# First-layer attention heads placed between value chunks, logarithm-based normalisations and per-tile waits in a two-layer decoder kernel

## The chip, the cores and the metric

The kernel runs on one core of one Trainium2 chip. The metric is the device time of one execution in microseconds (us). The times of before are three runs; a separate execution was profiled, and all rows come from it.

## The reference

Two decoder layers over 512 tokens of width 1024, four heads of 256, everything in float32. The part that the change touches is the attention of layer 0 (stick-breaking), the output projections and the layer normalisations:

```python
# layer 0, per head, s < t only
z = (q @ k.T) / 16
log_1m = where(mask, -softplus(z), 0)
tail = sum over j > s of log_1m[t, j]
a = where(mask, exp(log_sigmoid(z) + tail), 0)
mix = (a @ v) @ w_o
x = layer_norm(alpha * x + mix) * g + b        # three such norms before the last
x = layer_norm(alpha * x + feed_forward(x)) * g + b
x = x + (p @ w_proj) * sigmoid(x @ w_gate)
```

Layer 1 computes a softmax attention with a forget-gate bias, then a top-2-of-8 expert feed-forward with routing.

## The kernel before

All products are made of fp32r halves: a tensor is split into a rounded part (`_hi`) and the remainder (`_lo`), and `mm3` (L706 to L711) issues three matmuls per product. ScalarE (ACT) makes the `_hi` copy, VectorE (DVE) the `_lo` remainder, of weights and of results alike. Weights arrive in chunks through four `raw` buffers on the SP queue (a load waits for the `lo_ready` of the chunk four before it) and are split into two buffers `w_hi`/`w_lo`; chunk c+1 can be split when chunk c-1 has been used.

The phases run in the order of the list `PHASES`: `q0`, `k0`, `v0` (the three projections of layer 0), then the heads of layer 0, `o0` (its output projection), norm 0, `gu` and `down` (feed-forward), norm 1 with the embedding projection `proj0`, `gate0`, then `q1`, `k1`, the heads of layer 1 with the value chunks `v1` between them, `o1`, norm 2, routing, experts, the last gate. Each of `q0`, `k0`, `v0`, `o0`, `q1`, `k1`, `v1`, `o1` has eight chunks. For q, k, o a chunk is one feature tile of 128 (8 x 3 matmuls of 512 columns); for v two chunks make 256 value features (48 matmuls of 256 columns each).

**Heads of layer 0** (TensorE part L866 to L921). The triangle of scores of one head is four key tiles n = 3, 2, 1, 0 of 128, 256, 384 and 512 query columns, in PSUM banks 3 to 0. `scores_a` makes z; ACT computes Abs, Exp and Ln of it into `ln_a` (L1387 to L1392), DVE adds max(z, 0) and multiplies the diagonal blocks by the 0/1 tile `keep` (L1821, L1828); ACT and DVE split the result into `sp_hi`, `sp_lo`; `tails_a` (L891, L895) adds the reverse sums in the same banks; DVE clips the diagonal blocks with `floor_a` (L1838), ACT takes Exp (L1401, L1403), DVE makes `a_hi` and `a_lo` (L1844, L1622), and `mix_a` multiplies by the values. The tiles of this work (`ln_a`, `sp`, `a_hi` and so on) lie in the memory of `x_hi` and `x_lo`, which `v0` reads. TensorE's order is: all of `v0`; scores of head 0; then for each head its tails, the scores of the next head, its mix; then a wait for all eight mixed tiles, and `o0`.

**Heads of layer 1** have the other order already: value chunk 2h, turning the weights of head h, value chunk 2h+1, scores of head h+1, mix of head h. There the causal mask is added in PSUM by one matmul of an identity (`turn_r`) with a tile of large negative numbers (`mask_r`, L987).

**Norms** (ACT from L1305, DVE from L1710). The mean is a matmul (L809, L810), DVE subtracts it, ACT squares (L1311), TensorE averages the squares (L817), ACT takes the square root (L1319), DVE the reciprocal (L1719). Per feature tile DVE multiplies by it (L1725); then ACT writes `x_hi` with gain and bias (L1302) and `x_exact` with gain and bias (L1303), and DVE subtracts the two into `x_lo`. The first two chunks of `gu`, `gate0` and `q1` consume these tiles as they arrive. In norm 1 the splits of `proj0` and `gate0` weights are written between these steps by hand.

In `k1` the DVE step `sides` (L1896 to L1909), five operations on the gate sums and four that make the per-head tiles, sits after the drain of chunk 4. The order on each engine is written out by hand; semaphores alone join the engines.

## Time and profile before

| what | value |
|---|---|
| three runs, median (lowest, highest) | 1445.09 us (1443.63, 1447.59) |
| profiled execution, its time | 1448.43 us |
| its span | 1446.7 us |
| mean granted TensorE clock | 0.956 of full |
| TensorE busy | 1316.7 us, 91% of the span |

The span runs from the first to the last recorded instruction. In a stream of matmuls a row's duration overlaps the next one, so the distance between two starts is what a matmul costs. "Idle before" is the time that an engine stood still, and the arrow names what ended it. A duration of 0.39 us for a 512-column matmul goes with a distance of 0.23 us (clock 2.4 GHz), 0.63 us with 0.43 us (1.2 GHz).

### The profile page before, as it was taken

How to read it: one execution, taken by the hardware profiler on the slowest of the kernel's cores; microseconds unless marked ns; L12 is line 12 of the kernel's file. 1: busy time of each engine (PE TensorE's matmuls, PEld its weight loads, DVE VectorE, ACT ScalarE, POOL GpSimd, SP SyncE). 2: the span in 40 equal slices, each digit the busy share in tenths (PEclk: the TensorE clock that was granted, in tenths of full speed). 3: DMA queues.
4: the chain of work that ended last, by engine and by line, in shares of the span. 5: the costliest groups of instructions: out<-in, count | busy, mean ns of one | idle time of the engine just before them, and what ended most of it. 6: DMA issues, size and time to landing. Idle time of an engine off the chain costs nothing.

```text
span 1446.7 us, 17484 instructions
## 1 busy us (share of the span) xinstructions
PE 1316.7 (91%) x6495; PEld 1102.9 (76%) x6496; DVE 638.7 (44%) x870; ACT 562.2 (39%) x771; POOL 149.7 (10%) x106
## 2 busy tenths in 40 slices
PE   7999879799999999998899999988799899988658
PEld 6889778488888878876786899756687799866547
DVE  5333554633333323336533455344643643354465
ACT  3222552632223222126322233233544644555632
POOL 0000000000000000000000000000333533344400
PEclk9999899999999999999999999997899999988869
DMA  7332003033333333212346431211875866588831
GB/s 187 106 102 78 26 5 98 29 102 87 102 101 87 112 100 100 87 36 74 102 78 65 91 59 44 80 44 73 249 239 173 291 234 196 174 265 261 307 146 59
DMA packets 197911, 175.45 MB, mean 121 GB/s; under 512 B 7200, under 2 KB 178272, under 8 KB 197856
## 3 DMA queue, kind: packets, MB, share of 16 engines
q1 hardware_dynamic: 194016, 160.53, 38.6%
q0 software_dynamic: 3312, 12.06, 2.2%
q10 hardware_dynamic: 528, 2.10, 0.4%
q8 instruction: 37, 0.61, 0.2%
q14 instruction: 18, 0.15, 0.0%
HBM read 164.71 MB, written 9.96 MB: 121 GB/s over the span
## 4 chain that ended last, share of the span: by engine, by line
PE 81%; DVE 6%; issue 6%; ACT 4%; POOL 2%; DMA 1%; POOLq 0%; ACTq 0%; SPq 0%; DVEq 0%
PE bank L709 25%; PE bank L711 24%; PE bank L710 24%; PE bank L817 1%; POOL w_lo L667 1%; DVE w_lo L1622 1%; DVE rstd L1719 1%; PE bank L1026 1%; DMA raw<-moe_w_down 1%; PE bank L891 1%; DMA x_tok<-x 1%; PE bank L895 1%; DVE sp L1821 0%; PE bank L953 0%; DVE a_lo L1622 0%
## 5 line engine op out<-in xcount | busy, mean ns | idle before, releaser
L1622 DVE TENSOR_TENSOR w_lo<-raw,w_hi 128x1024 fp32r<-128x1024 f32 (+5 forms) x215 | 300.4, 1403 | 315.2 <-ACT w_hi L1222 157.5
L709 PE MATMUL bank<-x_hi,w_hi 128*128 128x512 f32 x672 | 265.4, 395 | 17.6 <-DVE x_lo L1622 11.4
L711 PE MATMUL bank<-x_hi,w_lo 128*128 128x512 f32 x672 | 264.0, 393 | 0.0
L710 PE MATMUL bank<-x_lo,w_hi 128*128 128x512 f32 x672 | 263.8, 393 | 0.0
L1222 ACT CAST w_hi<-raw 128x1024 fp32r<-128x1024 f32 (+2 forms) x141 | 149.7, 1063 | 157.5 <-PE bank L711 150.9
L709 PE MATMUL bank<-w_hi,x_hi 128*128 128x256 f32 (+2 forms) x608 | 189.0, 311 | 8.5 <-DVE x_lo L1650 3.2
L710 PE MATMUL bank<-w_lo,x_hi 128*128 128x256 f32 (+2 forms) x608 | 186.5, 307 | 0.0
L711 PE MATMUL bank<-w_hi,x_lo 128*128 128x256 f32 (+2 forms) x608 | 186.4, 307 | 0.0
L709 PEld LDWEIGHTS bank<-x_hi,w_hi 128*128 128x128 f32 x672 | 127.6, 190 | 49.2 <-DVE w_lo L1622 12.1
L1510 ACT CAST w_hi<-raw 128x1536 fp32r<-128x1536 f32 (+2 forms) x98 | 130.3, 1339 | 75.1 <-PE bank L711 47.3
L711 PEld LDWEIGHTS bank<-x_hi,w_lo 128*128 128x128 f32 x672 | 127.4, 190 | 27.2
L710 PEld LDWEIGHTS bank<-x_lo,w_hi 128*128 128x128 f32 x672 | 127.7, 190 | 26.0
L709 PEld LDWEIGHTS bank<-w_hi,x_hi 128*128 128x128 f32 x608 | 115.9, 191 | 12.9 <-issue 9.6
L667 POOL TENSOR_TENSOR w_lo<-raw,w_hi 128x1536 fp32r<-128x1536 f32 (+2 forms) x33 | 103.7, 3141 | 181.4 <-ACT w_hi L1510 136.4
L710 PEld LDWEIGHTS bank<-w_lo,x_hi 128*128 128x128 f32 x608 | 116.0, 191 | 0.0
L711 PEld LDWEIGHTS bank<-w_hi,x_lo 128*128 128x128 f32 x608 | 115.9, 191 | 0.0
L635 POOL IOTA lane_ids<- 128x128 f32 x1 | 0.2, 238 | 910.5 <-DVE q_lo L1650 910.5
L709 PE MATMUL bank<-w_hi,het_hi 128*128 128x512 f32 x132 | 63.0, 477 | 13.4 <-POOL w_lo L667 6.6
L709 PE MATMUL bank<-h_hi,w_hi 128*128 128x512 f32 x176 | 69.3, 394 | 3.2 <-DVE h_lo L1622 3.2
L710 PE MATMUL bank<-h_lo,w_hi 128*128 128x512 f32 x176 | 69.1, 393 | 0.0
L711 PE MATMUL bank<-h_hi,w_lo 128*128 128x512 f32 x176 | 69.0, 392 | 0.0
L1280 ACT CAST x_hi<-x_exact 128x512 fp32r<-128x512 f32 (+1 forms) x24 | 14.9, 621 | 118.1 <-DVE x_exact L1687 118.1
(298 smaller groups left out, 1864.1 us busy)
## 6 DMA issues: line engine op xcount, KB each, us to landing
raw<-moe_w_gu SPq DMA_DIRECT2D x32, 768.0 KB, 4.6
raw<-ffn_w_gu SPq DMA_DIRECT2D x44, 512.0 KB, 3.8
raw<-moe_w_gu SPq DMA_DIRECT2D x32, 640.0 KB, 4.2
raw<-a_w_qkv SPq DMA_DIRECT2D x24, 512.0 KB, 3.7
raw<-moe_w_down SPq DMA_DIRECT2D x16, 768.0 KB
raw<-ffn_w_down SPq DMA_DIRECT2D x16, 704.0 KB, 4.4
raw<-ple_w_gate SPq DMA_DIRECT2D x16, 512.0 KB, 4.1
raw<-kvf_w SPq DMA_DIRECT2D x16, 512.0 KB, 6.9
```

The costliest lines, as they stand in the source:

```text
L667: op = pool.tensor_tensor(w_lo[j][:, 0:n], raw[j][:, 0:n], w_hi[j][:, 0:n].bitcast(F32), ALU.subtract)
L709: pe.matmul(o, s_hi, m_hi, start=start, stop=False, skip_group_check=True)
L710: pe.matmul(o, s_hi, m_lo, start=False, stop=False, skip_group_check=True)
L711: return pe.matmul(o, s_lo, m_hi, start=False, stop=stop, skip_group_check=True)
L817: pe.matmul(bank[5][:, :], mean_f[:, :], sq[k % 2][:, :], start=k == 0, stop=k == KD - 1).then_inc(var_done, 1)
L891: mm = pe.matmul(bank[n][:, 0:WID[n]], neg_incl[:, :], part[:, OFF[n]:OFF[n] + WID[n]], start=False, stop=n == TT - 1 and part is sp_lo, s ...
L895: mm = pe.matmul(bank[n][:, (m - n) * P:WID[n]], neg_ones[:, :], part[:, OFF[m]:OFF[m] + WID[m]], start=False, stop=m == TT - 1 and part i ...
L1026: mm = pe.matmul(bank[5][0:NE, :], w_r[:, k, :], x_exact[:, k, :], start=k == 0, stop=k == KD - 1)
L1222: act.copy(w_hi[j % 2][:, 0:n], raw[j][:, 0:n]).then_inc(hi_ready, 1)
L1280: act.copy(x_hi[:, k, :], x_exact[:, k, :]).then_inc(y_hi_ready, 1)
L1510: op = act.copy(w_hi[j][:, 0:n], raw[j][:, 0:n])
L1622: return dve.tensor_tensor(dst, a, b, ALU.subtract)
```

## The change

- Layer 0's heads take the order of layer 1: `scores_a(0)` follows `k0`; then for each head value chunk 2h, its tails, value chunk 2h+1, the scores of the next head, its mix. The tiles of the head work move out of `x_hi`/`x_lo`, into the part of `q`/`k` memory of the head that is done with it; `ln_a` and `sp_wide` lie in other scratch memory.
- The mask of layer 0 is one more 128-column matmul per score tile (16 in all); the multiplications by `keep` and the clip by `floor_a` are gone. DVE prepares `turn_r` and `mask_r` between `q0` and `k0`.
- Value results: half a group is signalled early (`v_half`), in both layers.
- Norms 0 to 2: square root and reciprocal become Ln (L1319) and Exp with scale -0.5, both on ACT; the table load ahead of the squares stays in norm 1 alone. In norms 0 and 1 the gain goes into the DVE multiplication and the bias into `x_hi` (ACT) and `x_lo` (DVE); `x_exact` gets its bias later: in norm 0 by eight ACT operations within the first four chunks of `gu`, in norm 1 within the gate's addition (DVE).
- `o0` and `o1` wait for each mixed tile ahead of its own first use, in place of one wait for all eight.
- The load of `p` moves behind the loads of `gu` on the SP queue; in `k1` the four per-head operations move from after chunk 4 to after chunk 5.

The diff, cut to its core, with the common indentation taken off:

```diff
@@ -303,16 +306,10 @@
-wk = lambda name, shape, dt, o: at(name, shape, dt, work0 + o)
-ln_a = wk("ln_a", [P, TRI], F32, 0)
-sp = wk("sp", [P, TRI], F32, 5 * KB)
-sp_hi = wk("sp_hi", [P, TRI], R32, 10 * KB)
-sp_lo = wk("sp_lo", [P, TRI], R32, 15 * KB)
-a_hi = wk("a_hi", [P, TRI], R32, 20 * KB)
-a_lo = wk("a_lo", [P, TRI], R32, 25 * KB)
-a_diag = wk("a_diag", [P, TT, P], F32, 30 * KB)
...
+narrow = [[at(f"narrow{h}_{i}", [P, TRI - SEQ], R32, G + 4 * h * KB + 16 * i * KB) for i in range(2)] for h in range(H)]
+wide = [[at(f"wide{h}_{i}", [P, SEQ], R32, G + 4 * h * KB + 32 * KB + 2 * i * KB) for i in range(2)] for h in range(H)]
+sp_narrow = [at(f"sp_narrow{h}", [P, TRI - SEQ], F32, G + 4 * h * KB + 48 * KB) for h in range(H)]
@@ -530,11 +528,11 @@
-load_p(0)
...
+load_p(0)
@@ -765,6 +763,8 @@
+            if mixed_before is not None and isinstance(i, int) and i == j == 0:
+                pe.wait_ge(mix_lo, mixed_before + k + 1)
@@ -773,33 +773,20 @@
-def value_chunk(c):
...
-    weights(BASE["v1"] // RAW + c // RAW, c % RAW)
-    if c and c % 2 == 0:
-        pe.wait_ge(v_ready, 2 * (c // 2))
+def value_chunk(l, c):
...
+    weights(BASE[VALUES[l]] // RAW + c // RAW, c % RAW)
+    if c % 2 == 0 and (l or c):
+        pe.wait_ge(v_ready, 2 * H * l + 2 * (c // 2))
...
+        if t == 1 and c % 2:
+            mm.then_inc(v_half, 1)
...
-def values(name):
...
-    def step(q, i, j, last):
-        weights(q, j)
-        if j % 2 == 0:
-            free_of(DRAINED[name] + (0 if i == 0 and j == 0 else 4 * i + j - 2))
-        for t in range(TT):
-            for k in range(4):
-                w, kk = slice(k * 256, (k + 1) * 256), j % 2 * 4 + k
-                mm = mm3(bank[j // 2 * 4 + t][:, 0:256], x_hi[:, kk, t * P:(t + 1) * P],
-                         x_lo[:, kk, t * P:(t + 1) * P], w_hi[j % 2][:, w], w_lo[j % 2][:, w],
-                         kk == 0, kk == KD - 1)
-        mm.then_inc(chunk_done, 1)
-    quads(pe, name, step)
@@ -867,18 +854,24 @@
-values("v0")
...
 def scores_a(h):
...
+        else:
+            pe.wait_ge(drained, DRAINED["k0"] + 4 + g + 1)
+            pe.wait_ge(masks, 1)
...
-            mm = mm3(bank[n][:, 0:WID[n]], k_hi[:, f, n * P:(n + 1) * P], k_lo[:, f, n * P:(n + 1) * P],
-                     q_hi[:, f, n * P:], q_lo[:, f, n * P:], d == 0, d == DT - 1)
-        mm.then_inc(z_done, 1)
+            mm3(bank[g][:, 0:WID[n]], k_hi[:, f, n * P:(n + 1) * P], k_lo[:, f, n * P:(n + 1) * P],
+                q_hi[:, f, n * P:], q_lo[:, f, n * P:], d == 0, False)
+        pe.matmul(bank[g][:, 0:P], turn_r[:, :], mask_r[:, :], start=False, stop=True,
+                  skip_group_check=True).then_inc(z_done, 1)
...
+def sp_part(h, n, i):
+    return narrow[h][i][:, OFF[n] - SEQ:OFF[n] - SEQ + WID[n]] if n else wide[h][i][:, :]
...
 def tails_a(h):
@@ -904,21 +896,21 @@
-            a = slice(OFF[n], OFF[n] + WID[n])
-            mm = mm3(bank[6 + d][:, n * P:], v_hi[:, n, c], v_lo[:, n, c], a_hi[:, a], a_lo[:, a],
+            if d == 0 and n % 2 == 0:
+                pe.wait_ge(v_ready, 2 * h + n // 2 + 1)
+            mm = mm3(bank[6 + d][:, n * P:], v_hi[:, n, c], v_lo[:, n, c], sp_part(h, n, 0), sp_part(h, n, 1),
...
-        mm.then_inc(mixed, 1)
...
-pe.wait_ge(drained, DRAINED["o0"] - 2)
+    mm.then_inc(mixed, DT)
...
+    value_chunk(0, 2 * h)
...
+    value_chunk(0, 2 * h + 1)
...
-pe.wait_ge(mix_lo, KD)
-tiles("o0", q_hi, q_lo)
+tiles("o0", q_hi, q_lo, mixed_before=0)
@@ -1251,28 +1242,19 @@
-def split_value(c):
-    c += BASE["v1"]
-    split_hi(c // RAW, c % RAW, SIZE["v1"])
...
-def value_hi(g):
...
-    act.wait_ge(chunk_done, BASE["v1"] + 2 * g + 2)
+def split_value(l, c):
+    c += BASE[VALUES[l]]
+    split_hi(c // RAW, c % RAW, KD * P)
...
+def value_hi(l, g):
...
+        if b:
+            act.wait_ge(chunk_done, BASE[VALUES[l]] + 2 * g + 2)
+        else:
+            act.wait_ge(v_half, H * l + g + 1)
...
-def values_hi(name):
-    def step(q, i, j, last):
-        ahead(name, q, j, last)
-        if j % 2 == 0:
-            return
-        act.wait_ge(chunk_done, 4 * q + j + 1)
-        g = 2 * i + j // 2
-        for t in range(TT):
-            op = act.copy(v_hi[:, t, g * 256:(g + 1) * 256], bank[j // 2 * 4 + t][:, 0:256])
-        op.then_inc(out_hi, 2)
-    quads(act, name, step, peel=True)
@@ -1298,12 +1280,19 @@
 def affine_tile(n, k):
...
-    if n != 2:
-        act.activation(x_hi[:, k, :], x_exact[:, k, :], ACT.Identity, bias=b, scale=g)
-    act.activation(x_exact[:, k, :], x_exact[:, k, :], ACT.Identity, bias=b, scale=g).then_inc(affine, 1)
+    if n == 2:
+        act.activation(x_exact[:, k, :], x_exact[:, k, :], ACT.Identity, bias=b, scale=g).then_inc(affine, 1)
+    else:
+        act.activation(x_hi[:, k, :], x_exact[:, k, :], ACT.Identity, bias=b).then_inc(shifted, 1)
...
+def shift_exact(k):
...
+    act.activation(x_exact[:, k, :], x_exact[:, k, :], ACT.Identity,
+                   bias=ln_cols[:, 32 + k:33 + k]).then_inc(affine, 1)
...
 def norm(n):
-    act.preload_act_table_set("sqrt_and_others")
+    if n == 1:
+        act.preload_act_table_set("natural_log_exp_and_others")
@@ -1316,7 +1305,9 @@
-    act.activation(rstd[:, :], bank[5][:, :], ACT.Sqrt, bias=eps[:, 0:1]).then_inc(std_ready, 1)
+    act.activation(rstd[:, :], bank[5][:, :], ACT.Ln, bias=eps[:, 0:1]).then_inc(std_ready, 1)
+    act.wait_ge(std_ready, n + 1)
+    act.activation(rstd[:, :], rstd[:, :], ACT.Exp, scale=-0.5).then_inc(rstd_ready, 1)
@@ -1365,49 +1356,54 @@
-values_hi("v0")
...
-def mix_high(h):
...
+def mix_high(l, h):
...
+    act.wait_ge(mixed, KD * l + DT * (h + 1))
...
-        act.wait_ge(mixed, DT * h + d + 1)
-        act.copy(q_hi[:, DT * (h % H) + d, :], bank[6 + d][:, :]).then_inc(mix_hi, 1)
+        act.copy(q_hi[:, DT * h + d, :], bank[6 + d][:, :]).then_inc(mix_hi, 1)
...
-act.wait_ge(drained, DRAINED["o0"])
...
-    for g, group in enumerate(((3, 2, 1), (0,))):
-        lo, hi = OFF[group[-1]], OFF[group[0]] + WID[group[0]]
-        if h and g == 0:
...
-            act.wait_ge(a_lo_ready, 2 * h)
+    if h:
+        value_hi(0, h - 1)
+        act.wait_ge(a_lo_ready, 2 * h)
+    parts = ((3, 2, 1), (0,))
+    for g, group in enumerate(parts):
...
-            op = act.activation(ln_a[:, OFF[n]:OFF[n] + WID[n]], bank[n][:, 0:WID[n]], ACT.Abs)
+            op = act.activation(ln_a[:, OFF[n]:OFF[n] + WID[n]], bank[TT - 1 - n][:, 0:WID[n]], ACT.Abs)
...
+    for g, (lo, hi) in enumerate(((SEQ, TRI), (0, SEQ))):
...
-    for g, (lo, hi) in enumerate(((OFF[1], TRI), (0, OFF[1]))):
-        act.wait_ge(sp_ready, 2 * h + g + 1)
-        act.copy(sp_hi[:, lo:hi], sp[:, lo:hi]).then_inc(sp_hi_ready, 1)
+    split_value(0, 2 * h + 1)
+    act.wait_ge(sp_ready, 2 * h + 1)
+    act.copy(narrow[h][0][:, :], sp_narrow[h][:, :]).then_inc(sp_hi_ready, 1)
+    act.wait_ge(sp_ready, 2 * h + 2)
+    act.copy(wide[h][0][:, :], sp_wide[:, :]).then_inc(sp_hi_ready, 1)
...
-        mix_high(h - 1)
+        mix_high(0, h - 1)
...
-        act.wait_ge(diag_cut, TT * h + g + 1)
-        op = act.activation(ln_a[:, OFF[n]:OFF[n] + P], a_diag[:, n, :], ACT.Exp)
-        if n < TT - 1:
-            op = act.activation(ln_a[:, OFF[n] + P:OFF[n] + WID[n]], bank[n][:, P:WID[n]], ACT.Exp)
-        op.then_inc(a_ready, 1)
-mix_high(H - 1)
+        act.wait_ge(tail_done, TT * h + g + 1)
+        act.activation(ln_a[:, OFF[n]:OFF[n] + WID[n]], bank[g][:, 0:WID[n]], ACT.Exp).then_inc(a_ready, 1)
+    split_value(0, 2 * h + 2)
+value_hi(0, H - 1)
+second_early("o0")
+mix_high(0, H - 1)
...
 def gu_step(q, i, j, last):
...
+    if isinstance(i, int) and i == 0:
+        act.wait_ge(x_ready, KD)
+        shift_exact(2 * j)
+        shift_exact(2 * j + 1)
@@ -1703,6 +1685,7 @@
+            dve.wait_ge(affine, KD)
@@ -1715,20 +1698,25 @@
-    dve.wait_ge(std_ready, n + 1)
-    dve.reciprocal(rstd[:, :], rstd[:, :]).then_inc(rstd_ready, 1)
...
     def scale(k):
-        dve.tensor_tensor(x_exact[:, k, :], x_exact[:, k, :], rstd[:, :], ALU.mult).then_inc(normed, 1)
+        if n == 2:
+            dve.tensor_tensor(x_exact[:, k, :], x_exact[:, k, :], rstd[:, :], ALU.mult).then_inc(normed, 1)
+        else:
+            dve.scalar_tensor_tensor(out=x_exact[:, k, :], in0=x_exact[:, k, :],
+                                     scalar=ln_cols[:, n * KD + k:n * KD + k + 1], in1=rstd[:, :],
+                                     op0=ALU.mult, op1=ALU.mult).then_inc(normed, 1)
...
     def low_tile(k):
...
-            dve.wait_ge(affine, done + k + 1)
-            minus(x_lo[:, k, :], x_exact[:, k, :], x_hi[:, k, :].bitcast(F32)).then_inc(x_ready, 1)
+            dve.wait_ge(shifted, KD * n + k + 1)
+            dve.scalar_tensor_tensor(out=x_lo[:, k, :], in0=x_exact[:, k, :],
+                                     scalar=ln_cols[:, 32 + n * KD + k:33 + n * KD + k],
+                                     in1=x_hi[:, k, :].bitcast(F32), op0=ALU.add, op1=ALU.subtract
+                                     ).then_inc(x_ready, 1)
@@ -1776,12 +1764,14 @@
-        dve.tensor_tensor(x_exact[:, k, :], x_exact[:, k, :], proj[:, k, :], ALU.add).then_inc(embedded, 1)
+        dve.scalar_tensor_tensor(out=x_exact[:, k, :], in0=x_exact[:, k, :],
+                                 scalar=ln_cols[:, 32 + KD + k:33 + KD + k], in1=proj[:, k, :],
+                                 op0=ALU.add, op1=ALU.add).then_inc(embedded, 1)
...
-            dve.wait_ge(affine, 2 * KD + k + 1)
+            dve.wait_ge(affine, KD + k + 1)
@@ -1813,37 +1803,31 @@
+    if h:
+        value_lo(0, h - 1)
...
-        lo, hi = OFF[group[-1]], OFF[group[0]] + WID[group[0]]
...
-            o = slice(OFF[n], OFF[n] + WID[n])
-            op = dve.scalar_tensor_tensor(out=sp[:, o], in0=bank[n][:, 0:WID[n]], scalar=0.0, in1=ln_a[:, o],
-                                          op0=ALU.max, op1=ALU.add)
-        op.then_inc(sp_raw, 1)
-        dve.wait_ge(sp_raw, 2 * h + g + 1)
...
-        for n in group:
-            o = slice(OFF[n], OFF[n] + P)
-            op = dve.tensor_tensor(sp[:, o], sp[:, o], keep[:, :], ALU.mult)
+            dst = sp_narrow[h][:, OFF[n] - SEQ:OFF[n] - SEQ + WID[n]] if n else sp_wide[:, :]
+            op = dve.scalar_tensor_tensor(out=dst, in0=bank[TT - 1 - n][:, 0:WID[n]], scalar=0.0,
+                                          in1=ln_a[:, OFF[n]:OFF[n] + WID[n]], op0=ALU.max, op1=ALU.add)
...
-    for g, (lo, hi) in enumerate(((OFF[1], TRI), (0, OFF[1]))):
+    split_value(0, 2 * h + 1)
+    for g, (part, full) in enumerate(((narrow[h], sp_narrow[h]), (wide[h], sp_wide))):
...
-        minus(sp_lo[:, lo:hi], sp[:, lo:hi], sp_hi[:, lo:hi].bitcast(F32)).then_inc(sp_lo_ready, 1)
+        minus(part[1][:, :], full[:, :], part[0][:, :].bitcast(F32)).then_inc(sp_lo_ready, 1)
...
-    for g, n in enumerate(reversed(range(TT))):
-        dve.wait_ge(tail_done, TT * h + g + 1)
...
-        dve.tensor_tensor(a_diag[:, n, :], bank[n][:, 0:P], floor_a[:, :], ALU.min).then_inc(diag_cut, 1)
-    if h:
...
-        dve.wait_ge(mixed, DT * h)
-    for g, (lo, hi) in enumerate(((OFF[1], TRI), (0, OFF[1]))):
+    for g, (part, lo, hi) in enumerate(((narrow[h], SEQ, TRI), (wide[h], 0, SEQ))):
...
-        dve.tensor_copy(a_hi[:, lo:hi], ln_a[:, lo:hi]).then_inc(a_hi_ready, 1)
+        if g == 0:
+            dve.wait_ge(tail_done, TT * (h + 1))
+        dve.tensor_copy(part[0][:, :], ln_a[:, lo:hi]).then_inc(a_hi_ready, 1)
...
-        minus(a_lo[:, lo:hi], ln_a[:, lo:hi], a_hi[:, lo:hi].bitcast(F32)).then_inc(a_lo_ready, 1)
+        minus(part[1][:, :], ln_a[:, lo:hi], part[0][:, :].bitcast(F32)).then_inc(a_lo_ready, 1)
+    split_value(0, 2 * h + 2)
+value_lo(0, H - 1)
+second_early("o0")
@@ -1903,12 +1887,14 @@
+def head_sides():
...
-tiles_lo("k1", k_hi, k_lo, between={1: gate_sums, 2: gate_lows, 4: sides})
+tiles_lo("k1", k_hi, k_lo, between={1: gate_sums, 2: gate_lows, 4: sides, 5: head_sides})
```

## Rows read from the trace of the kernel before

**Rows 1.** The page: the chain that ended last, shares of the span by engine.

```profile
PE 81%; DVE 6%; issue 6%; ACT 4%; POOL 2%; DMA 1%; POOLq 0%; ACTq 0%; SPq 0%; DVEq 0%
```

**Rows 2.** Stretches: length, busy PE, PEld, DVE, ACT, POOL; PEclk, DMA share, GB/s.

```profile
102.70:150.35 47.65, 46.15 (x385) 46.18 (x386) 14.47 (x21) 12.14 (x21) 0.00 (x0) 1.00 0.30 92
150.35:165.00 14.65, 9.28 (x47) 8.48 (x46) 6.52 (x17) 9.66 (x20) 0.00 (x0) 0.79 0.01 2
```

**Rows 3.** Timeline of PE, layer 0: start, duration, what [idle before].

```profile
104.20 0.36 PE L709 MATMUL bank<-w_hi,x_hi 128*128 128x256 f32 x1 [1.50 <-DVE k_lo L1650]
...
150.35 0.22 PE L709 MATMUL bank<-q_hi,k_hi 128*128 128x128 f32 x1
...
153.93 0.40 PE L711 MATMUL bank<-q_hi,k_lo 128*128 128x512 f32 x1
159.70 0.48 PE L891 MATMUL bank<-sp_hi,neg_incl 128*128 128x128 f32 x1 [5.37 <-DVE sp_lo L1622]
...
213.32 0.50 PE L709 MATMUL bank<-q_hi,w_hi 128*128 128x512 f32 x1 [1.40 <-DVE q_lo L1650]
```

**Rows 4.** The chain in order of time: tails of head 2, first and last.

```profile
188.06 0.73 PE bank L891 x4
...
190.28 0.78 PE bank L895 x6
```

**Rows 5.** Busy time by stretch, heads of layer 1.

```profile
846.00:866.00 20.00, 20.00 (x157) 19.42 (x155) 9.69 (x20) 7.09 (x15) 0.00 (x0) 1.00 0.35 59
```

**Rows 6.** Timeline of PE, layer 1: start of the last mix, start of `o1`.

```profile
908.61 0.47 PE L709 MATMUL bank<-wt,v_hi 128*128 128x512 f32 x1 [1.49 <-DVE v_lo L1650]
...
914.64 0.50 PE L709 MATMUL bank<-q_hi,w_hi 128*128 128x512 f32 x1 [2.00 <-DVE q_lo L1650]
```

**Rows 7.** Timeline of ACT, then of DVE, head 0 of layer 0.

```profile
151.76 1.28 ACT L1377 ACT_TABLE_LOAD   x1
...
154.20 0.84 ACT L1390 ACTIVATE ln_a<-ln_a 128x768 f32<-128x768 f32 x1
...
155.82 0.58 ACT L1387 ACTIVATE ln_a<-bank 128x512 f32<-128x512 f32 x1
...
158.69 1.55 DVE L1622 TENSOR_TENSOR sp_lo<-sp,sp_hi 128x768 fp32r<-128x768 f32 x2
```

**Rows 8.** Timeline at norm 0 and the start of `gu`: ACT, DVE, PE.

```profile
269.94 0.69 ACT L1319 ACTIVATE rstd<-bank,eps 128x512 f32<-128x512 f32 x1 [0.28 <-PE bank L817]
...
285.54 0.80 ACT L1303 ACTIVATE x_exact<-x_exact,ln_cols 128x512 f32<-128x512 f32 x1
288.17 1.05 ACT L1222 CAST w_hi<-raw 128x1024 fp32r<-128x1024 f32 x1 [1.83 <-PE bank L711]
...
293.85 1.23 DVE L1622 TENSOR_TENSOR w_lo<-raw,w_hi 128x1024 fp32r<-128x1024 f32 x1 [0.19 <-ACT w_hi L1222]
...
277.33 0.76 PE L709 MATMUL bank<-x_hi,w_hi 128*128 128x512 f32 x1 [7.43 <-DVE x_lo L1622]
```

**Rows 9.** Stretch from the first `gu` matmul: length, busy PE, and so on.

```profile
277.33:295.90 18.57, 18.57 (x72) 13.93 (x73) 11.55 (x16) 13.51 (x18) 0.00 (x0) 0.88 0.10 29
```

**Rows 10.** DVE groups by line, the whole span: count, busy, mean ns.

```profile
L1719 DVE RECIPROCAL rstd<-rstd 128x512 f32<-128x512 f32 x3 | 10.1, 3350 | 5.7 <-ACT rstd L1319 5.7
...
L1725 DVE TENSOR_TENSOR x_exact<-x_exact,rstd 128x512 f32<-128x512 f32 x24 | 15.6, 685 | 0.1
...
L2134 DVE SCALAR_TENSOR_TENSOR y_two<-y_one,row_stats,b_row 128x512 f32<-128x512 f32 x8 | 5.7, 749 | 0.1
```

**Rows 11.** Timeline at norm 1: ACT, then PE's first matmul of `gate0`.

```profile
670.09 1.99 ACT L1222 CAST w_hi<-raw 128x1024 fp32r<-128x1024 f32 x2
...
673.58 0.50 PE L709 MATMUL bank<-x_hi,w_hi 128*128 128x512 f32 x1 [4.26 <-DVE w_lo L1622]
```

**Rows 12.** Timeline in `k1`: the per-head operations (DVE), and PE's wait.

```profile
811.35 1.68 DVE L1908 TENSOR_SCALAR s_side<-s_all,head_rows 128x512 fp32r<-128x512 f32 x4
...
814.21 0.50 PE L709 MATMUL bank<-x_hi,w_hi 128*128 128x512 f32 x1 [1.97 <-DVE w_lo L1622]
```

96 lines of the change are left out of this document (42 added, 54 removed).

## The prediction

> **What bounds the kernel now.** I read the chain that ended last first: 81% of it is TensorE [rows 1], so the time changes where TensorE's own work or a wait in front of it changes. Then I went through the stages. `v0` keeps TensorE busy for 46.15 of 47.65 us at full clock [rows 2], or 5.76 us for each of its eight chunks, after one wait of 1.50 us for the last key tile [rows 3]. The heads of layer 0 do not: the first score matmul starts at 150.35, and `o0` starts at 213.32 [rows 3], 63.0 us for four heads. After the first scores TensorE waits 5.37 us for `sp_lo` [rows 3], and in the stretch with that wait the granted clock is 0.79 [rows 2]: the work after the gap runs at 1.2 GHz. In layer 1, where value chunks stand between the heads, 20.00 of 20.00 us are busy at clock 1.00 [rows 5]. That pair of stretches is the heart of the case.
>
> **Part 1, the heads between the value chunks.** What TensorE itself needs at 2.4 GHz, per head: two value chunks, 11.52 us; scores, 150.35 to 153.93 plus the 0.23 of the last, 3.8 us [rows 3]; tails, 188.06 to 191.06, 3.0 us [rows 4]; mix, from 908.61 to the 2.00 us of idle ahead of 914.64, 4.0 us, less some 0.15 by which the last row reaches over [rows 6], 3.9 us. The four mask matmuls are new to layer 0; each has 128 columns and costs between 0.06 (a quarter of the 0.23 of 512 columns) and 0.13 (the six of 128 to 384 columns that end the tails take 0.78 [rows 4]); I take 0.1, nearer to the row, so 0.4. Sum 22.6 us per head, 90.4 for four. From 102.70 (the 104.20 start less its idle 1.50 [rows 3]) this reaches 193.1.
>
> Two waits stay. The first is in head 0, where only one value chunk covers the chain from the last score to `sp_lo`. Before, that chain waited 5.37 us. Now ACT runs Abs of all tiles first, then Exp and Ln of both parts, then the split of a value chunk, then the copy; DVE has that chunk's remainder ahead of its own. From the end of the scores: 0.2 latency, Abs 0.58, Exp and Ln narrow 2 x 0.85, both wide 2 x 0.63 [rows 7], chunk copy 1.05 [rows 8], then on DVE the chunk's remainder, 1.23 in its row [rows 8], and half of the 1.55 pair with its start, 0.9 [rows 7]: about 7.0 us against 5.76. I take a stall of 1.3. In heads 1 to 3 the cover is mix plus chunk, 3.9 + 5.76 = 9.7, and the chain ends 2.6 us early, so no stall. The table load of 1.28 [rows 7] and the two mask copies on DVE are hidden behind 3.8 us of scores and a k chunk of 5.5 us (24 matmuls at 0.23); uncovered they would cost 1.3 and 0.4. The second wait is the last mix, for the second half of the values: in layer 1 the mix waited 1.49 us for both halves [rows 6]; now the first half comes early, the first six matmuls of the mix (512 and 384 columns) give 1.2 us of cover, and about 0.4 us is left. So `o0` starts at 193.1 + 1.3 + 0.4 = 194.8 without its own wait (six ready feature tiles, 18 matmuls, cover 4.1 us; the last two tiles need 2.3). It started at 213.32: **18.5 us saved**. The bounds: 20.2 without either wait; 9 if heads 1 to 3 each wait 3 us more than this.
>
> The removed DVE work (`keep`, `floor_a`) was on the old chain and is hidden in the new one. The load of `p` is moved past all loads of `v0`, `o0` and `gu` on SP's queue; it is first needed after `down`, and the share of the DMA engines in use is 0.30 [rows 2]. It costs nothing as long as loads run several chunks ahead; without that cover it costs one landing, a few us.
>
> **Part 2, `o1` and the last mix of layer 1.** The 2.00 us wait ahead of `o1` goes, and of the 1.49 us 0.3 stays [rows 6]: **3.2 us saved**.
>
> **Part 3, `k1`.** The four per-head operations, 1.68 us, sat ahead of the remainder of chunk 6, and TensorE waited 1.97 us for it [rows 12]. Moved past it, they sit beside a chunk of 5.5 us with some 3 us to spare: **1.6 us saved**, 0.4 stays.
>
> **Part 4, the norms.** The reciprocal takes 3.35 us, three times [rows 10]; in its place ACT runs an Exp like the 0.69 us Ln [rows 8], plus 0.15 to signal DVE. That is 2.5 us per norm. Norm 2 saves **2.5**.
> Norm 0: besides, `x_exact` (0.71 from start to start, 0.80 in its row [rows 8]) no longer lies between `x_hi` and `x_lo`, but three multiplications do now end after it, so 0.4 to 0.7 comes on top; and DVE's operations become scalar_tensor_tensor with two SBUF sources and a pointer: the same form costs 749 ns where a tensor_tensor costs 685 [rows 10], four times 0.06 in front. The first `gu` matmul comes 2.9 us earlier. After it TensorE is the limit, as before (72 matmuls in 18.57 us without idle [rows 9]). But the biases of `x_exact` now stand on ACT in `gu`: four of them, 2.84 us, between the copy of chunk 2 and the first Silu, and chunk 3's split is queued behind that Silu. That split ends now at 293.85 + 1.23 = 295.08 [rows 8], with TensorE free for it at 296.1 [rows 9], a slack of 1.0. The new stall is 1.8. Norm 0 saves **1.1** (bounds 0, if a table load falls in between too, and 3.5).
> Norm 1: `gate0` does not wait for the norm, but for its own weights, 4.26 us [rows 11], whose copies (1.99 us from 670.09) stand behind four pairs of ACT operations. Four `x_exact` operations fall away, 2.8 us, then the copy of the second chunk waits for `proj0`'s last chunk, done at 669.3 (673.58 less 4.26 [rows 11]). That makes **1.5** (bounds 0.5 and 3).
>
> **Sum.** 18.5 + 3.2 + 1.6 + 2.5 + 1.1 + 1.5 = 28.4 us. The profiled execution took 1448.43 (span 1446.7 and 1.7 around it): 1420.0. The median of the runs shown is 3.3 lower, 1445.09, and the same saving gives **1416.7**.
>
> **The rivals.**
> *A, heads that stall.* Each head's chain passes some ten operations on ACT and as many on DVE; if queued value copies or splits make heads 1 to 3 wait as head 0 does (1.3) or as long as 3 us, the saving falls by 4 to 9: 1420 to 1426. For it: ACT's order is fixed and mixes both kinds of work. Against: 2.6 us of slack by my count, and layer 1, with the same splits, does not wait [rows 5].
> *B, slow DVE operations.* If scalar_tensor_tensor with two float32 sources from SBUF ran at half the rate (1.37 us for 512), the 32 of norms 0 and 1 would be the limit of the first two chunks behind each: a pair 2.6 us against TensorE's 1.37 per tile. Norm 0 would end 8 us later and norm 1 some 4, and `q1` 0.7: 1429. Rows of that form at 749 ns speak plainly against it [rows 10]. This is what the Trainium skill states (Vector Engine (DVE) Microarchitecture Reference, section "7. Points that are easy to get wrong"): the form with two non-bf16 SBUF sources halves throughput. The trace does not agree: 749 beside 685 ns.
> *C, table loads come back.* Squares and Identity ran under the square-root table so far; no row shows them under the log/exp table. If each norm needed two loads of 1.28 us [rows 7] in its chain, 7.7 us would be lost: 1424. The Trainium skill (ScalarE: Activation LUTs, "Table sets: the hidden batching unit") says that cheap functions such as identity and abs are in every set; Abs and copies under the log/exp table agree, squares stay open.
> *D, slower.* The interleaved region of 90 us draws TensorE at 1.2 GHz. A 512-column matmul then costs 0.43 against 0.23, so each us becomes 1.87, and the saving is gone when 33 of the 90 us run so. All of it: 78 us more, 1495. What speaks for it: the old heads did run partly at half clock [rows 2]. Against: that followed 5.4 us of idle, and layer 1's same pattern holds 1.00 [rows 5], while waits of 1.49 and 2.00 us [rows 6] were followed by matmuls at full rate.
> *E, more than the sum.* The bias operations on ACT may cost no stall, and shorter gaps in norms 0 and 1 (7.43 and 4.26 us now [rows 8, 11]) may keep the clock up, 1.5 us each: 1411 or 1412.
> *F, the change does not do what it says.* TensorE's scores could be held by `masks` or by a bank of `k0`. Scores use banks 0 to 3 in the order in which `k0` drains them, and the masks are made a whole phase earlier, so at most 1.5 us returns: inside the forecast.
>
> **How the numbers follow.** The forecast has 0.70, A 0.10, B 0.03, C 0.04, D 0.02, E 0.10; 0.01 is left for something else that takes the gain. A measurement of this kernel tells 0.3%, 4.3 us, from no change. All but D and part of the rest lie far beyond it: faster 0.96, same 0.02, slower 0.02. The range goes from E's 1411, less 2 for the spread between runs, to A's 1426: 1409 to 1426.
>
> **What would show it.** Right: between the end of `k0` and `o0` some 92 us, PE idle there below 2.5 us, clock 1.00, one wait for `sp_lo` of about 1 us in head 0; no reciprocal of 3.35 us; the first `gu` matmul 3 us sooner after the last square; a wait of 1 to 2 us at chunk 3 of `gu`; no wait ahead of `o1`; 0.4 us in `k1`. Wrong: `sp_lo` waits in every head (A), x_lo rows of 1.4 us (B), table loads around the squares (C), or a granted clock well below 1 between 103 and 195 us (D).

## The result, and the profile after

The changed kernel takes 1408.56 us in the median of 4 runs (1405.77 to 1415.48), the kernel before beside it 1444.36 us (4 runs, 1443.47 to 1447.59): ratio 0.9755, 95% interval 0.9716 to 0.9795. I had forecast 1416.7 us, range 1409 to 1426. It is faster, as forecast, and the median lies 0.44 us below the range. Three more measurements of the same kernel, shown below, gave medians of 1406.71, 1410.77 and 1406.10 us, so the forecast was 6 to 11 us too slow.

The profiled execution took 1415.48 us (span 1413.8, granted clock 0.963), the slowest of the four. Its chain of waits, shares by engine:

```profile
PE 84%; DVE 4%; issue 4%; DMA 3%; ACT 3%; POOL 1%; ACTq 0%; SPq 0%; POOLq 0%; DVEq 0%
```

TensorE (PE) sets the time more than before (81%, [rows 1]). Its timeline at the places of the forecast, start, duration, what, [idle before]:

```profile
103.89 0.22 PE L707 MATMUL bank<-q_hi,k_hi 128*128 128x128 f32 x1
114.81 0.44 PE L884 MATMUL bank<-narrow,neg_incl 128*128 128x128 f32 x2 [0.75 <-DVE narrow L1612]
192.18 0.39 PE L707 MATMUL bank<-narrow,v_hi 128*128 128x256 f32 x1 [0.18 <-DVE v_lo L1640]
194.84 0.45 PE L707 MATMUL bank<-q_hi,w_hi 128*128 128x512 f32 x1
255.68 0.70 PE L707 MATMUL bank<-x_hi,w_hi 128*128 128x512 f32 x1 [4.31 <-DVE x_lo L1716]
275.22 0.50 PE L707 MATMUL bank<-x_hi,w_hi 128*128 128x512 f32 x1 [1.04 <-DVE w_lo L1612]
650.22 0.50 PE L707 MATMUL bank<-x_hi,w_hi 128*128 128x512 f32 x1 [2.45 <-DVE w_lo L1612]
699.71 0.77 PE L707 MATMUL bank<-x_hi,w_hi 128*128 128x512 f32 x1 [4.03 <-DVE x_lo L1612]
788.08 0.50 PE L707 MATMUL bank<-x_hi,w_hi 128*128 128x512 f32 x1 [0.39 <-DVE w_lo L1612]
882.38 0.39 PE L707 MATMUL bank<-wt,v_hi 128*128 128x256 f32 x1 [0.18 <-DVE v_lo L1640]
885.02 0.45 PE L707 MATMUL bank<-q_hi,w_hi 128*128 128x512 f32 x1
944.57 8.73 PE L1017 MATMUL bank<-x_exact,w_r 128*8 128x512 f32 x16 [3.01 <-ACT x_exact L1284]
```

Read it against [rows 3, 6, 8, 11, 12]. The heads' 5.37 us wait is 0.75, the last mix waits 0.18 in layer 0 and 0.18 in layer 1 (1.49 before), and there is no wait ahead of `o0` (194.84) or `o1` (885.02). The wait ahead of `gu` went from 7.43 to 4.31, ahead of `gate0` from 4.26 to 2.45, in `k1` from 1.97 to 0.39. New is 1.04 us at the fourth `gu` chunk. Busy time from the first score matmul to `o0` (length, PE, PEld, DVE, ACT, POOL; clock, DMA share, GB/s):

```profile
103.89:194.84 90.95, 90.02 (x674) 87.08 (x672) 43.31 (x64) 47.75 (x81) 0.00 (x0) 1.00 0.17 49
```

The groups by line (count, busy, mean ns, idle before) for VectorE (DVE) and then ScalarE (ACT):

```profile
L1708 DVE SCALAR_TENSOR_TENSOR x_exact<-x_exact,ln_cols,rstd 128x512 f32<-128x512 f32 x16 | 11.7, 747 | 1.8 <-ACT rstd L1310 1.8
L1716 DVE SCALAR_TENSOR_TENSOR x_lo<-x_exact,ln_cols,x_hi 128x512 fp32r<-128x512 f32 x16 | 11.6, 746 | 0.0
L1706 DVE TENSOR_TENSOR x_exact<-x_exact,rstd 128x512 f32<-128x512 f32 x8 | 4.9, 683 | 5.7 <-ACT rstd L1310 5.7
```

```profile
L1308 ACT ACTIVATE rstd<-bank,eps 128x512 f32<-128x512 f32 x3 | 2.1, 688 | 2.2 <-PE bank L804 2.2
L1310 ACT ACTIVATE rstd<-rstd 128x512 f32<-128x512 f32 x3 | 1.9, 631 | 0.1
```

**Where the time went.** The program has waypoints on TensorE that every run shares. Where no stretch at the lower clock is longer or shorter, the lengths between them repeat so well that a difference of 0.5 us can be read. They are differences of starts in the timelines, in us, and "norm" is the first of the matmuls that average the squares (L817 before, L804 after); the first column runs from the third group of transposes of `x_tok`, since that start moves by 1 us with the loads.

| profile | to o0 | o0 to norm 0 | norm 0 to gu | gu to down | to norm 1 | norm 1 to gate0 | gate0 to q1 | q1 to o1 | norm 2 to router | router to second proj | proj to end |
|---|---|---|---|---|---|---|---|---|---|---|---|
| before | 202.00 | 48.88 | 15.13 | 245.18 | 127.59 | 23.48 | 49.48 | 191.58 | 13.44 | 28.15 | 441.6 |
| before_again | 205.16 | 48.87 | 15.14 | 245.18 | 127.58 | 23.49 | 49.44 | 191.47 | 13.44 | 28.14 | 434.8 |
| before_warm | 196.38 | 48.90 | 15.14 | 245.24 | 128.72 | 23.50 | 47.82 | 190.46 | 13.44 | 26.57 | 435.5 |
| after | 182.34 | 48.83 | 12.01 | 246.07 | 127.40 | 21.07 | 49.49 | 185.31 | 10.71 | 27.53 | 441.7 |
| after_again | 182.55 | 48.82 | 12.01 | 246.03 | 127.57 | 21.07 | 47.94 | 186.27 | 10.71 | 25.32 | 434.2 |
| after_third | 182.12 | 48.83 | 12.00 | 246.06 | 127.35 | 21.07 | 49.51 | 185.28 | 10.72 | 27.59 | 437.6 |
| after_fourth | 182.66 | 48.81 | 12.01 | 246.13 | 127.52 | 21.07 | 47.91 | 186.30 | 10.72 | 25.28 | 441.8 |
| values_first | 201.67 | 48.84 | 12.01 | 246.11 | 127.39 | 21.07 | 49.52 | 185.33 | 10.71 | 27.60 | 432.3 |
| values_warm | 194.69 | 48.81 | 12.01 | 246.88 | 127.58 | 21.07 | 47.90 | 186.55 | 10.72 | 26.09 | 437.9 |
| recip | 183.10 | 48.83 | 14.90 | 246.50 | 127.57 | 21.48 | 47.90 | 186.27 | 13.44 | 30.09 | 434.1 |
| two_identity | 182.04 | 48.83 | 12.23 | 245.93 | 128.73 | 22.75 | 49.98 | 186.64 | 10.71 | 28.07 | 433.0 |
| small_undone | 184.62 | 50.49 | 12.01 | 246.13 | 127.29 | 21.07 | 49.50 | 188.97 | 10.71 | 26.74 | 436.0 |
| small_again | 184.65 | 50.48 | 12.01 | 246.12 | 127.41 | 21.06 | 49.52 | 189.06 | 10.71 | 26.72 | 438.4 |
| small_warm | 184.07 | 48.93 | 12.01 | 246.10 | 127.52 | 21.08 | 47.90 | 190.06 | 10.72 | 28.90 | 444.1 |
| bias_late | 182.89 | 48.82 | 12.01 | 248.16 | 125.95 | 21.07 | 49.54 | 185.32 | 10.72 | 27.50 | 435.8 |
| warm | 181.97 | 48.83 | 12.01 | 246.10 | 128.81 | 21.06 | 47.89 | 183.81 | 10.72 | 25.05 | 438.7 |
| bias_last_warm | 182.38 | 48.83 | 12.01 | 244.73 | 127.57 | 21.06 | 47.87 | 183.85 | 10.71 | 25.20 | 438.5 |
| best_again | 181.89 | 48.83 | 12.00 | 245.76 | 128.85 | 21.09 | 47.89 | 183.88 | 10.71 | 25.08 | 438.8 |

(`o1` to norm 2 is 48.8 to 48.9 everywhere.) Before less after, in the two profiles shown first: 19.66 to `o0`, 0.05, 3.12 and -0.89 around norm 0, 0.19, 2.41, -0.01, 6.27, 2.73, 0.62. With a start that is 1.2 us later and a last part that is alike by chance this is the 32.9 us between the spans. What follows the second projection (experts and last gate) takes 435 to 442 us in three profiles of the kernel before and its variant, and 432 to 444 us in those of the changed kernel and its variants: that is the scatter, and nothing of the gain.

### The profile page after: what moved, and what is told of

It reads as the page before. It is cut to its first block, busy times and chain, and to the rows that moved or that the text cites. A ratio compares the mean times of both kernels' runs of the same rounds, so it can differ in the third digit from the quotient of the medians.

```text
span 1413.8 us, 17461 instructions
## 1 busy us (share of the span) xinstructions
PE 1308.8 (93%) x6511; PEld 1098.7 (78%) x6512; DVE 623.3 (44%) x829; ACT 552.4 (39%) x743; POOL 149.5 (11%) x106
## 4 chain that ended last, share of the span: by engine, by line
PE 84%; DVE 4%; issue 4%; DMA 3%; ACT 3%; POOL 1%; ACTq 0%; SPq 0%; POOLq 0%; DVEq 0%
PE bank L707 26%; PE bank L708 25%; PE bank L709 25%; DMA raw<-moe_w_down 2%; PE bank L804 2%; DVE w_lo L1612 1%; POOL w_lo L665 1%; DMA x_tok<-x 1%; ACT w_hi L1500 1%; PE bank L1017 1%; PE bank L945 0%; PE bank L884 0%; DVE het_lo L1640 0%; PE bank L797 0%; PE bank L796 0%
## 5 line engine op out<-in xcount | busy, mean ns | idle before, releaser
L707 PEld LDWEIGHTS bank<-x_hi,w_hi 128*128 128x128 f32 x672 | 127.1, 189 | 43.6 <-DVE w_lo L1612 10.2
```

The source lines that it names most:

```text
L707: pe.matmul(o, s_hi, m_hi, start=start, stop=False, skip_group_check=True)
```

## The experiments

Times are medians. Four groups of runs were measured, each on one chip together with 11 runs of the kernel before (median in brackets): after_again, values_first, recip, warm (1445.39); two_identity, small_undone, bias_late, before_again (1444.40), without the changed kernel beside them; before_warm, values_warm, bias_last_warm, after_third (1446.13); small_again, small_warm, best_again, after_fourth (1445.33). "Low clock" in us is 2 x (1 - granted clock) x length, summed over stretches: the time at 1.2 GHz.

**1. The two kernels again.** No edit.

> The changed kernel once more, unaltered, in five rounds. Theory A (every term of the sum was cut a little too small, and the changed kernel is really some 36 us faster than the kernel before): ratio 0.973 to 0.977, median 1406 to 1411 us, and a second profile shows the same landmarks as the first within 0.5 us for the heads (90.9 us from the first score matmul to o0) and for each gap of the norms (4.3, 2.5, 4.0, 3.0 us). Rival B (the 0.44 us by which the result passed the range is scatter of the granted clock alone, and the sum of 28.4 us was right): median 1414 to 1418 us, ratio 0.980 or above.

> The kernel before, unaltered, for a second profile of it. If the part of the time from the first matmul of the second per-layer projection to the end (441.6 us before; 441.7 and 434.2 us in two profiles of the changed kernel) is scatter that both kernels have, it comes out anywhere from 432 to 443 us here, while the part ahead of it stays within 1.5 us of 1005.1 us. If it is fixed for a kernel, it is 441 to 442 us again.

Measured: the changed kernel 1406.71 us (1404.21 to 1412.32), ratio 0.9737 (0.9712 to 0.9762). Theory A stands, B falls. In the third and fourth measurement (below) the ratios are 0.9745 (0.9712 to 0.9777) and 0.9726 (0.9692 to 0.9760). The second profile of the kernel before has 434.8 us behind the second projection: scatter, as expected. But ahead of it that projection starts at 1008.99, not within 1.5 us of 1005.1: 0.9 us is the start, and 3.2 us lie in the heads, whose waits sum to 14.2 and 14.7 us. The stretches of the heads (all of them, then that behind the wait of 1.42 us at 174.45, then the next two heads), and the same of the second profile:

```profile
154.00:213.00 59.00, 45.11 (x250) 41.53 (x248) 35.29 (x80) 34.64 (x75) 0.00 (x0) 0.88 0.00 1
...
175.00:182.00 7.00, 7.00 (x39) 6.70 (x38) 4.53 (x10) 2.41 (x10) 0.00 (x0) 0.76 0.00 0
182.00:206.00 24.00, 18.28 (x116) 16.76 (x114) 17.30 (x40) 16.85 (x37) 0.00 (x0) 1.00 0.00 1
```

```profile
154.00:217.00 63.00, 48.66 (x253) 44.67 (x251) 35.52 (x80) 35.60 (x77) 0.00 (x0) 0.84 0.00 1
```

Clock 0.88 and 0.84: 14 and 20 us at the lower level behind waits of 1.4 to 5.4 us, where the heads of the changed kernel have 1.00.

**2. The value chunks back ahead of the heads.**

```diff
+for c in range(2 * H):
+    value_chunk(0, c)
 scores_a(0)
+pe.wait_ge(v_ready, 2 * H)
 for h in range(H):
-    value_chunk(0, 2 * h)
     tails_a(h)
-    value_chunk(0, 2 * h + 1)
...
```

Left out here: the chunks use two pairs of banks in turn, as before, and ScalarE's and VectorE's work on them moves ahead of the heads.

> The changed kernel with the value chunks of layer 0 all ahead of the first head, in two pairs of banks as before, everything else kept. If the interleaving alone is what Part 1 gained, it is slower than the changed kernel by 18.5 us (my sum) to 19.8 us (the two profiles), 1427 to 1429 us. If the shorter chain of a head (mask in the matmul instead of two rounds of VectorE work, Exp of a whole tile at once) brought a share of it, 13 to 17 us, 1422 to 1425 us, with head periods without chunks under the 15 us of [rows 2 and 3]. If the chunks were hidden anyway, under 5 us.

Measured: 1427.45 us (1420.13 to 1429.94), 20.7 us behind after_again. All the gain of Part 1 is the interleaving; the shorter chain of a head brings nothing. The waits are those of before:

```profile
159.78 1.19 PE L888 MATMUL bank<-narrow,neg_incl 128*128 128x128 f32 x4 [5.36 <-DVE narrow L1619]
176.91 0.73 PE L888 MATMUL bank<-narrow,neg_incl 128*128 128x128 f32 x4 [1.45 <-DVE narrow L1619]
189.44 0.72 PE L888 MATMUL bank<-narrow,neg_incl 128*128 128x128 f32 x4 [1.44 <-DVE narrow L1619]
203.55 0.72 PE L888 MATMUL bank<-narrow,neg_incl 128*128 128x128 f32 x4 [1.44 <-DVE narrow L1619]
209.30 0.50 PE L711 MATMUL bank<-wide,v_hi 128*128 128x512 f32 x1 [2.78 <-DVE wide L1619]
```

They sum to 12.5 us (0.93 in the changed kernel); the way to `o0` is 19.0 to 19.6 us longer (201.67 against 182.12 to 182.66). The rest is low clock, 17.0 us of it up to 260 us.

**3. TensorE kept busy in the waits.** `warm` puts matmuls that nobody reads into waits; where a part of the wait is left behind them in the profile (0.2 to 0.8 us), they ended before it did.

```diff
+def warm(b, count, src):
+    for _ in range(count):
+        pe.matmul(bank[b][:, :], neg_ones[:, :], src[:, 0, 0:SEQ], start=True, stop=True)
```

In the heads of values_first:

> The run with the value chunks ahead of the heads, with the same matmuls in the waits of the heads (20, 5, 5, 5 and 11). If the interleaving's 20.7 us are 12.5 us of waits and the rest lower clock behind them (17.0 us at the lower level up to 260 us in that profile), this one stands 12 to 14 us behind the changed kernel and 6 to 8 us ahead of the run without the added matmuls, 1420 us. If the interleaving gains in another way (less contention, shorter heads), it stays at 1427 us.

In the kernel before:

> The kernel before with matmuls that nobody reads in TensorE's waits: 20, 5, 5 and 5 ahead of the tails of the four heads of layer 0, 11 ahead of the last mix, 5 ahead of o0, 29 ahead of gu, 16 ahead of gate0, 15 ahead of q1, 7 ahead of o1 and 23 ahead of the router matmul; the waits themselves stay. The two profiles of this kernel show 13.6 and 27.3 us at the lower granted clock up to 300 us, 10.2 and 10.3 us between 640 and 940. Theory (the waits cost their own length and a stretch at the lower clock behind them, which my sum left out): these stretches go, o0 starts at 207 to 210 us instead of 213.3 and 217.4, and the whole is faster than the kernel before by 6 to 12 us. Rival (the low clock behind the waits lies beside work of VectorE that sets the end, so it costs nothing): within 3 us.

In the changed kernel:

> The changed kernel with matmuls that nobody reads put into the waits of TensorE ahead of gu (16), gate0 (8), q1 (15) and the router matmul (12), 128x512 each, in banks that are free there. If the granted clock falls to its lower level because TensorE idled there (2.3 us at 0.51 behind the gap of gu, 2.3 at 0.50 behind that of q1, 3.0 at 0.65 behind that of gate0), these stretches go back to 1.00 and the kernel is faster by half of the 3.4, 3.4 and 3.2 us at the lower level, 4 to 5 us in all, and the spread of its runs shrinks. If the clock falls by a budget of its own and only shifts, or the added matmuls delay the first ones of the stage, 0 to 3 us slower.

Measured. before_warm: 1435.57 us (1430.15 to 1438.34), 10.6 us faster than the kernel before (ratio 0.9915, 0.9884 to 0.9946), within the 6 to 12 of the theory. In its profile the way to `o0` is 5.6 and 8.8 us shorter than in the two without, and no low clock is left up to 300 us (20.5 us in the first profile of the kernel before, 27.3 in the second; the 13.6 of the expectation are those ahead of `o0` alone):

```profile
154.00:208.00 54.00, 51.27 (x302) 45.24 (x302) 34.86 (x80) 34.91 (x77) 0.00 (x0) 1.00 0.00 1
```

values_warm: its profile agrees, to `o0` 7.0 us shorter than values_first and 12.0 to 12.6 behind the changed kernel, about the sum of the waits. Its median does not: 1427.78 (1422.40 to 1434.78), 17.0 us behind the changed kernel beside it where 12 to 14 were expected, the profiled run being the fastest. I can't say what the other five did. warm: 1407.72 us, no faster than after_again, where 4 to 5 us were expected. There four waits are filled, and the two halves of the claim part. Ahead of `gu` the clock stays up, but nothing is gained (12.01 + 246.10 against 12.01 + 246.03): TensorE then waits for each `x_lo`, which VectorE and ScalarE make every 1.33 us:

```profile
255.04 0.47 PE L707 MATMUL bank<-x_hi,w_hi 128*128 128x512 f32 x1 [0.65 <-DVE x_lo L1726]
256.27 0.50 PE L707 MATMUL bank<-x_hi,w_hi 128*128 128x512 f32 x1 [0.30 <-DVE x_lo L1726]
257.60 0.50 PE L707 MATMUL bank<-x_hi,w_hi 128*128 128x512 f32 x1 [0.36 <-DVE x_lo L1726]
```

From `gate0` to `o1` it does gain, 231.7 against 234.2 to 234.8, and up to the second projection its profile is 2 to 4.5 us ahead of the four of the changed kernel. But from `down` to norm 1 it loses 1.2 to 1.5 (128.81 against 127.35 to 127.57), with 6.1 us at the lower level there in place of 3.0 to 3.4. The rival of the expectation, that the low clock only shifts, is thus not ruled out as a part of it: before_warm and best_again lose the same there, bias_last_warm does not, and two_identity does without any added matmul. The medians show no gain.

**4. The reciprocal back.** Sqrt with its table load on ScalarE, then `dve.reciprocal`, in all norms.

> The changed kernel with Sqrt on ScalarE and the reciprocal on VectorE back in all three normalisations, with the table load of each; nothing else changed. My sum put 2.5 us on it in norms 0 and 2 and 1.5 us in norm 1: slower by 6.5 us, gaps ahead of gu, gate0 and the router matmul longer by 2.5, 1.5 and 2.5 us. If it also draws longer stretches at the lower granted clock behind each gap, slower by 8 to 10 us. If the logarithm was hidden, under 1 us.

Measured: 1416.24 us (1414.20 to 1421.70), 9.5 us behind after_again. Its TensorE:

```profile
258.88 0.76 PE L707 MATMUL bank<-x_hi,w_hi 128*128 128x512 f32 x1 [7.20 <-DVE x_lo L1715]
654.43 0.50 PE L707 MATMUL bank<-x_hi,w_hi 128*128 128x512 f32 x1 [2.45 <-DVE w_lo L1609]
950.87 9.51 PE L1017 MATMUL bank<-x_exact,w_r 128*8 128x512 f32 x15 [5.74 <-ACT x_exact L1284]
```

The logarithm, with the table load that it saves, is worth 2.89 us at norm 0, 2.73 at norm 2, and 0.41 at norm 1, where `gate0` waits for its weights (2.45 in both kernels). That is 6.0; the remaining 3.5 are within what low clock behind longer gaps and scatter make (router to projection 30.09, the longest of all, with 19.8 us at the lower level against 10.0 to 13.3 in the changed kernel).

**5. Gain and bias as they were**, logarithm kept.

> The changed kernel with the gain and bias of norms 0 and 1 as they were (two Identity activations a tile on ScalarE, a plain multiply by rstd on VectorE, a plain subtraction for x_lo), logarithm kept. From the run with the reciprocal put back, the logarithm is worth 0.4 us ahead of gate0, where the two profiles of before and after differ by 2.4: if the shared-out gain and bias bring the rest, the first gate0 matmul comes 2.0 us later here, counted from the first square of norm 1. At norm 0 the reciprocal accounts for 2.9 of 3.1 us ahead of gu, so 0.2 us later there; the 1.0 us wait at the fourth gu chunk goes. In all 1 to 3 us slower than the changed kernel. Rival (VectorE sets the first gu chunks, and it gains from the plain subtraction): no slower, within 1 us.

Measured: 1409.00 us (1407.49 to 1411.59), on another chip than 1406.71, and within the changed kernel's own medians of 1406.10 to 1410.77: no difference shown. By waypoints: norm 1 to `gate0` 22.75, so 1.68 us of its 2.41 are the shared-out gain and bias and 0.4 the logarithm. Around norm 0 nearly nothing: they bring `gu` 0.22 sooner, and 0.1 to 0.2 is given back behind it; the wait at the fourth chunk is gone in this run.

**6. The small waits back.**

```diff
-tiles("o0", q_hi, q_lo, mixed_before=0)
+pe.wait_ge(mix_lo, KD)
+tiles("o0", q_hi, q_lo)
...
-between={1: gate_sums, 2: gate_lows, 4: sides, 5: head_sides}
+between={1: gate_sums, 2: gate_lows, 4: lambda: (sides(), head_sides())}
```

> The changed kernel with the single wait for all mix_lo ahead of o0 and of o1, and with the four multiplications of the sides back behind the fifth k1 tile. By my sum: the wait ahead of o1 comes back with 2.0 us less the 0.4 that the last mix may cover, the wait in k1 with 1.6 us; ahead of o0 1.4 us. Together 4 to 5 us slower, and in its profile 1.4, 2.0 and 2.0 us of idle TensorE at these places. If the order of the chunks already hides these waits (o0's first two chunks are now split ahead), under 2 us.

> The run with the single waits ahead of o0 and o1 and the sides behind the fifth k1 tile, once more. The waits came back as forecast (2.00, 2.00 and 1.97 us), 5.6 us over the changed kernel's own, its profile stood 7.9 us behind at the second projection of the layer inputs, and its median 11 to 15 us. If lower clock behind the waits is drawn in some executions and not in others, the median is again 8 to 14 us behind the changed kernel and the executions spread over 8 us or more. If the first median was chance, 5 to 6 us behind.

The wait ahead of `o1` is put back in the same way. With eight unread matmuls in the waits ahead of `o0` and `o1`:

> The same with eight unread matmuls in the wait ahead of o0 and in that ahead of o1, which stay 2.0 us long. If what these waits cost over their length is lower clock, this one stands 5 to 7 us behind the changed kernel, 3 us or more ahead of the run without the matmuls, and shows no lower clock between o0 and norm 0. If it is something else, no difference between the two.

Measured: 1421.53 (1416.21 to 1426.51), then 1419.15 us (1417.32 to 1423.88); small_warm 1415.14 (1413.65 to 1424.13); the changed kernel beside the last two 1406.10 (1403.11 to 1418.23). So 13 us and more, where my terms gave 4 to 5. The waits are as named, 2.00, 1.97 and 2.00:

```profile
196.76 0.50 PE L707 MATMUL bank<-q_hi,w_hi 128*128 128x512 f32 x1 [2.00 <-DVE q_lo L1642]
793.09 0.50 PE L707 MATMUL bank<-x_hi,w_hi 128*128 128x512 f32 x1 [1.97 <-DVE w_lo L1614]
892.22 0.50 PE L707 MATMUL bank<-q_hi,w_hi 128*128 128x512 f32 x1 [2.00 <-DVE q_lo L1642]
```

Behind the one at `o0` the clock falls, behind the equally long one at `o1` it does not, in both profiles; with the matmuls it does not fall at `o0` either (small_undone at `o0` and `o1`, then small_warm at `o0`). They don't lengthen the way from the last mix to `o0`: from behind its wait of 0.18 us it is 4.82 us with them and 4.81 without:

```profile
196.00:204.00 8.00, 7.24 (x25) 5.84 (x26) 0.71 (x2) 0.00 (x0) 0.00 (x0) 0.79 0.07 20
...
890.00:900.00 10.00, 8.00 (x36) 6.55 (x36) 2.17 (x3) 2.12 (x3) 0.45 (x3) 1.00 0.18 50
```

```profile
196.00:204.00 8.00, 7.88 (x35) 6.44 (x35) 0.99 (x2) 1.05 (x1) 0.00 (x0) 1.00 0.02 4
```

So `o0` to norm 0 takes 50.49 and 50.48 against 48.83: a 2.0 us wait that costs 3.7. Profiles account for 7 to 8 us (2.2, 1.7, and 2.7 to 3.7 from `q1` to `o1`); the medians say 13. What the other 6 us are stays open: small_warm took 4 of the 13 away, and its profiled run, at 1424.13 the slowest of its six, had 444.1 us in the last part.

**7. Where the bias additions stand.** First behind the hidden tiles of the first `gu` round, then in the last round, there with unread matmuls ahead of `gate0` (8) and `q1` (15).

> The changed kernel with the eight bias additions to x_exact behind the hidden tiles of the first gu round instead of ahead of them. If ScalarE's eight additions delay the split of the fourth gu chunk, its wait of 1.04 us goes and the kernel is faster by 1.0 us, the down projection starting 1.0 us sooner after norm 0. If that wait comes from VectorE, which is itself late with x_lo, it stays (0.8 to 1.1 us) and nothing changes.

> The changed kernel with the bias additions to x_exact in the last gu round instead of the first, and 8 and 15 unread matmuls in the waits ahead of gate0 and q1. Behind the hidden tiles of the first round the additions made the waits there longer (1.30 and 1.42 us); in the last round nothing is late, so the 1.04 us wait at the fourth gu chunk should go: from the first square of norm 0 to the down projection 257.0 us instead of 258.0. The stretch from q1 to norm 2 was 232.6 us with these matmuls against 235.1 and 234.1 without: 1.5 to 2.5 us. Together 2 to 4 us faster than the changed kernel. If the waits only move on, within 1 us of it.

> The changed kernel with the bias additions in the last gu round and unread matmuls ahead of gate0 and q1, once more: its profile was 4.2 to 7.0 us ahead of the changed kernel's three at the second projection, its median 1.6 to 5.7 us ahead. If that is a gain, 3 to 5 us ahead again on this chip; if scatter, within 1.5 us.

> The changed kernel unaltered, as the measure of the three others on the same chip: 1404 to 1412 us, median 1407 to 1410 us, its granted clock 0.966 to 0.972.

> The changed kernel unaltered, the measure of the three others: median 1406 to 1411 us.

Measured. bias_late: 1410.76 us, neither of the two outcomes expected: there are two waits where one was, and both are longer:

```profile
276.38 0.50 PE L707 MATMUL bank<-x_hi,w_hi 128*128 128x512 f32 x1 [1.30 <-DVE w_lo L1612]
...
288.97 0.49 PE L707 MATMUL bank<-x_hi,w_hi 128*128 128x512 f32 x1 [1.42 <-DVE w_lo L1612]
```

ScalarE now does four additions in one block ahead of the next splits (the rows of bias_late, then of the changed kernel, where the first four stand ahead of the table load and the first Silu):

```profile
271.56 2.56 ACT L1290 ACTIVATE x_exact<-x_exact,ln_cols 128x512 f32<-128x512 f32 x4
274.03 2.18 ACT L1213 CAST w_hi<-raw 128x1024 fp32r<-128x1024 f32 x2
```

```profile
267.05 2.56 ACT L1290 ACTIVATE x_exact<-x_exact,ln_cols 128x512 f32<-128x512 f32 x4
269.63 1.28 ACT L1411 ACT_TABLE_LOAD   x1
270.93 0.60 ACT L1411 ACTIVATE h_tmp<-bank 128x512 f32<-128x512 f32 x1
```

In the last round nothing waits for them, and the wait is gone: norm 0 to `down` 256.74 against 258.04 to 258.14 (257.76 in the second profile, best_again, with more low clock behind the gaps). That the bias additions on ScalarE make the wait is thus shown. The profiles of bias_last_warm and best_again have the second projection at 965.10 and 966.73 against 969.3 to 972.1. Their medians are 1405.07 beside after_third's 1410.77, and 1406.79 beside after_fourth's 1406.10, which by the expectation is scatter. By waypoints from the third group of transposes they are 4 to 7 and 2 to 5 us ahead there; by the medians that is not shown.

## Why the prediction was wrong

The mechanism of every part was right, and every term was too small. Profile against profile the way to the second projection shrank by 34.2 us where the sum says 28.4. Of the 5.8 missing, Part 1 has 1.2, Parts 2 and 3 1.4, norm 0 1.1, norm 1 0.9, norm 2 0.2, the stretch behind the router 0.6, and 0.3 lie elsewhere. By waypoints, with all two and four profiles:

- **Part 1, 18.5 forecast.** The section shrank by 19.6 us against the profile shown and by 22.7 against the second one (182.4 in the mean, 202.00 and 205.16). One wait for `sp_lo`, in head 0, and none after it, as forecast; rival A did not happen. From the first score matmul to `o0` I had 92.1 us and it took 90.95: TensorE's own work is 90.0, not 90.4, the wait in head 0 is 0.75 us, not 1.3 (the items that I listed for its chain add up to 6.9 us against 5.76, so to 1.2 already), and the last mix waits 0.18, not 0.4. What I had not seen: some 14 us of the gain are waits and the other 6 to 9 are low clock behind them (196.38 in before_warm). Since I took the start of `o0` from one profile, the 14 us of low clock of that execution were in my term; the second profile has 20.
- **Parts 2 and 3, 4.8 forecast.** `gate0` to `o1` shrank by 6.1 to 6.8 us. The three waits gave 4.9, their bare length (1.58 in `k1`, 2.00 at `o1`, 1.31 at the last mix). The other 1.2 to 1.9 are a shorter stretch at the lower clock around `gate0` and `q1`: between 640 and 940 us there are 10.2 us of low clock in both profiles of the kernel before, 6.8 in all four of the changed one, and 3.4 us at half the clock cost 1.7.
- **Norm 2, 2.5 forecast:** 2.73, by recip wholly the reciprocal's.
- **Norm 0, 1.1 forecast:** 2.2. The first `gu` matmul came 3.12 us sooner (2.9 forecast); the new wait exists, but is 1.04 us, not 1.8: the split that `gu` waits for ended 19.5 us behind the first `gu` matmul (DVE row at 273.94, 1.22 long), against 17.75 before [rows 8], so the additions pushed it by 1.7 us, not by the 2.84 of the sum. The four took 2.56 us, not 2.84, the copy ahead of them began 0.4 us sooner after the first `gu` matmul, and 0.3 us of idle ahead of the first Silu went.
- **Norm 1, 1.5 forecast:** 2.4. I gave it all to the weights' copies: right in kind (two_identity 1.7; the wait fell from 4.26 to 2.45), short in size. The rest is that `proj0` itself ended 0.6 us sooner after the start of norm 1 (18.6 in place of 19.2 us), of which recip gives 0.4 to the logarithm.
- **Behind the router, 0 forecast:** 0.6 to 2.9. There are 14.5 us of low clock there before and 10.0 to 13.3 after.

Together these make 34 to 40 us ahead of the last part, against 28.4.

The step that failed is the one that turns gaps into time: outside Part 1 I counted each shorter wait at its bare length and put the low clock at nothing. That "shorter gaps in norms 0 and 1 ... may keep the clock up, 1.5 us each" stood beside the sum as a rival with a chance of 0.10, and against rival D I wrote that waits of 1.49 and 2.00 us "were followed by matmuls at full rate". They were, in layer 1; in the heads of layer 0 a wait of 1.42 us was followed by 7 us at 0.76 ([rows 2] held only the first such stretch). What the runs show in its place is 1.2 to 1.9 us from `gate0` to `o1`, 0.6 to 2.9 behind the router, and a saving in the heads that depends by 3.2 us on which profile one starts from. With it failed the sizes of Part 1 (1.2), norm 0 (1.1) and norm 1 (0.9), as above. The details of E were also wrong: at norm 0 the kept-up clock gives nothing (warm), around `gate0` and `q1` it does. The second error is the range: 2 us for the spread between runs, where the last part of the changed kernel alone moves by 7.6. That the first median fell within 0.44 us of the range says little; the three later ones lie 2.3 us below its lower end, 1.8 us above it, and 2.9 us below it.

B fell at once: 746 ns for the form beside 683, the same ratio as [rows 10]. The rule of the Trainium skill (Vector Engine (DVE) Microarchitecture Reference, section "7. Points that are easy to get wrong") that this form with two non-bf16 SBUF sources halves the throughput does not hold in any row here. C fell: squares (24 of them, 630 ns each) and Identity run under the logarithm's table, and norms 0 and 2 have no load. The rule of the Trainium skill (ScalarE: Activation LUTs, "Table sets: the hidden batching unit") that cheap functions such as identity are in every set agrees with this. D fell: 1.00 from 103.89 to 194.84. F fell: the first score matmul starts at 103.89 without a wait, which is 102.70 [rows 3] and the 1.2 us of the later start.

## What to carry to other kernels

Price a wait of the engine that sets the time at its length plus the low clock that may follow it: here 12.5 us of waits in the heads cost 19 us, and one of 2.0 us cost 3.7 at one place and 2.0 at another. Before taking a low clock as a loss, ask who is late at that place: behind norm 0 VectorE paces the first chunks and the full clock was worth nothing. And compare kernels by waypoints in two profiles of each before trusting a difference of totals: sections repeat within 0.6 us, low clock apart, while the total of the changed kernel moves from 1402.81 to 1418.23.

## What was not expected of the hardware

- Six waits of the kernel before, the same within 0.32 us in both profiles, drew 14 us of low clock in one execution and 20 in the other; a 2.0 us wait drew it at `o0` and not at `o1`. The length of the wait alone does not decide it.
- Idle time filled with matmuls that nobody reads kept the clock at 1.00 in every head of before_warm and made the whole kernel 0.85% faster (ratio 0.9915, 0.9884 to 0.9946) with its waits in place.
- Behind the 2.45 us wait ahead of `gate0` the clock fell in two profiles (after, after_third) and stayed up in two (after_again, after_fourth), which were longer at the lower level around `q1` instead; the two cases differ by 1.6 us at `q1` and by 0.6 at `o1`.
